# 22 of 36 modulation units moved from TensorE matmuls to multiply-adds on VectorE

## The reference

```python
c_act = jax.nn.silu(c)
for i in range(DEPTH):
    mod = (c_act @ mod_w[i] + mod_b[i]).reshape(B, N_SUBLAYERS, 3, D)
    shift, scale, gate = mod[:, :, 0], mod[:, :, 1], mod[:, :, 2]
    h = modulate(rms_norm(x, norm_g[i, 0]), shift[:, 0], scale[:, 0])
    x = x + 0.5 * gate[:, 0, None, :] * swiglu(h, w_gate[i, 0], w_up[i, 0], w_down[i, 0])
    ...
```

## Time and profile before

| | |
|---|---|
| median of 3 runs | 2283.04 us (2282.78 to 2283.24) |
| time of the profiled execution | 2281.24 us |
| its span | 2279.9 us |
| PE busy | 2187.2 us, 96% |
| DVE busy | 1365.1 us, 60% |
| ACT busy | 1095.2 us, 48% |
| moved by DMA | 448.64 MB, 197 GB/s on average |

### The profile page before, as it was taken

How to read it: one execution, slowest core, us unless ns; L and a number is a source line. 1 busy time by engine, 2 the same in 40 slices (tenths; PEclk the granted TensorE clock), 3 DMA queues, 4 the chain that set the end, 5 groups by cost and what they waited for, 6 DMA issues and landing times.

```text
span 2279.9 us, 33539 instructions
## 1 busy us (share of the span) xinstructions
PE 2187.2 (96%) x14432; PEld 1894.0 (83%) x14432; DVE 1365.1 (60%) x1776; ACT 1095.2 (48%) x1242; POOL 85.2 (4%) x92
## 2 busy tenths in 40 slices
PE   7999998999999999999899999999999999999998
PEld 5997665898789877678689987898999887998996
DVE  4543666654554466656665455567787664677884
ACT  4443555543444345545544335644555457445552
POOL 1200010000000000000000011000000111000000
PEclk9999999999999999999999999999999999999999
DMA  9776672656657655536265555444655564436551
GB/s 353 264 265 254 223 269 74 234 200 265 218 193 258 258 199 201 211 125 226 75 222 186 187 212 201 146 139 166 203 184 186 169 233 137 169 138 207 182 185 55
DMA packets 274819, 448.64 MB, mean 197 GB/s; under 512 B 10816, under 2 KB 146304, under 8 KB 274416
## 3 DMA queue, kind: packets, MB, share of 16 engines
q1 hardware_dynamic: 270016, 429.07, 54.5%
q0 software_dynamic: 4368, 16.31, 2.0%
q10 hardware_dynamic: 288, 1.11, 0.1%
HBM read 445.40 MB, written 1.06 MB: 196 GB/s over the span
## 4 chain that ended last, share of the span: by engine, by line
PE 78%; ACT 5%; DVE 4%; issue 1%; DMA 0%; POOL 0%; ACTq 0%; SPq 0%; DVEq 0%; POOLq 0%
PE ps L1449 76%; DVE wlo L1875 1%; ACT whi L1670 1%; PE ps L1636 1%; PE ps L1603 1%; ACT S L1670 1%; ACT L1670 1%; ACT xs L1670 0%; PE ps L1593 0%; DMA raw<-in_fox_w_in 0%; ACT xhi L1670 0%; DVE S L2009 0%; DVE x L1911 0%; ACT PT L1670 0%; DVE xs L1904 0%
## 5 line engine op out<-in xcount | busy, mean ns | idle before, releaser
L1875 DVE TENSOR_TENSOR wlo<-raw,whi 128x2048 fp32r<-128x2048 f32 (+1 forms) x339 | 768.2, 2274 | 533.1 <-ACT whi L1670 532.8
L1670 ACT ACTIVATE whi<-raw 128x2048 fp32r<-128x2048 f32 (+1 forms) x339 | 640.8, 1895 | 412.6 <-PE ps L1449 370.9
L1449 PE MATMUL ps<-xhi,whi 128*128 128x256 f32 x2632 | 649.5, 287 | 8.4 <-DVE wlo L1875 3.5
L1449 PE MATMUL ps<-xhi,wlo 128*128 128x256 f32 x2632 | 642.8, 284 | 0.0
L1449 PEld LDWEIGHTS ps<-xhi,whi 128*128 128x128 f32 x2632 | 507.4, 193 | 26.4 <-issue 16.5
L1449 PEld LDWEIGHTS ps<-xhi,wlo 128*128 128x128 f32 x2632 | 507.6, 193 | 1.3 <-issue 1.0
L1449 PE MATMUL ps<-xlo,whi 128*128 128x256 f32 x2632 | 344.3, 283 | 0.1
L1449 PEld LDWEIGHTS ps<-xlo,whi 128*128 128x128 f32 x2632 | 327.6, 192 | 0.5 <-DVE xlo L1975 0.3
L1449 PE MATMUL ps<-whi,xhi 128*128 128x512 f32 x736 | 299.1, 406 | 17.3 <-ACT xhi L1670 11.0
L1449 PE MATMUL ps<-wlo,xhi 128*128 128x512 f32 x736 | 291.9, 397 | 0.0
L1449 PE MATMUL ps<-whi,hhi 128*128 128x512 f32 x528 | 209.5, 397 | 1.9 <-DVE rows L1899 1.0
(11 more groups left out here) (218 smaller groups left out, 1811.9 us busy)
## 6 DMA issues: line engine op xcount, KB each, us to landing
raw<-in_mod_w SPq DMA_DIRECT2D x72, 1024.0 KB, 8.1
raw<-in_w_in SPq DMA_DIRECT2D x52, 1024.0 KB, 4.9
raw<-in_ffn_w_gate SPq DMA_DIRECT2D x88, 512.0 KB, 5.9
raw<-in_ffn_w_up SPq DMA_DIRECT2D x88, 512.0 KB, 6.9
raw<-in_ffn_w_down SPq DMA_DIRECT2D x44, 1024.0 KB, 8.7
raw<-in_w_up SPq DMA_DIRECT2D x88, 512.0 KB, 4.8
raw<-in_dil_w_in SPq DMA_DIRECT2D x36, 1024.0 KB, 5.5
raw<-in_w_down SPq DMA_DIRECT2D x22, 1024.0 KB, 4.9
```

Source lines behind the costliest of these rows:

```text
L1449: return nc.tensor.matmul(o, lhs, rhs, start=start, stop=stop, skip_group_check=True)
L1670: return nc.scalar.activation(o, i, func, **kw)
L1875: V.tensor_tensor(wlo[:, s["c"], 0:s["n"]], raw[:, s["slot"], 0:s["n"]], whi[:, s["c"], 0:s["n"]].bitcast(F32), ALU.subtract).then_inc(sem ...
```

## The change

22 of the 36 units are no longer matmuls. Each of their pieces ("half" below) is used by DVE in four instructions, one a row block: the first of a unit multiplies 128 x 512 weights by the column of `csil` (`tensor_scalar`), the others multiply and add onto an accumulator (`scalar_tensor_tensor`). There are two accumulators `macc` by turns, which lie in `xs[:, 1, :]`. PE then sums the accumulator over the partitions: a shift or scale unit by four float32 matmuls with one column of ones, a gate unit by one with 128 columns of ones as before. The copy to `mrow` on ACT goes away for them, and so does the reduce on DVE.

The instructions of a half are queued up (`work`) and put behind the matmuls of pieces in the order of steps: two behind each `gateup` piece, three behind each `down`. The slot of a half is free after its fourth instruction. PE's sums are put one unit later (`acc_turns`).

The halves stand before the steps that they go with: one before each `gateup` but the first (q = 2 to 10 in stage (0,0)), and one before `down` 0, 1, 3, 4 and 6, as long as the stage has any. Stage (0,0) has seven such units, (0,1) and (1,0) seven each, (1,1) one. The mixers keep four and one units as matmuls behind their steps; the second mixer had five. The norms keep one each, as before.

The transposes of x wait for one half of `xs` at a time. Two tiles of the mixers (`ftm`, `rtm`) now share memory with others.

```diff
+        while pc["slot_free"] and pc["slot_free"][0] == "mod_acc" and self.count.get("mod_acc", 0) < pc["slot_free"][1]:
+            self.run_work(1)
         c = pc["c"] = self.n_conv % CONV
...
+        for entry in self.acc_turns:
+            entry[0] -= 1
+        while self.acc_turns and self.acc_turns[0][0] < 0:
+            self.acc_turns.pop(0)[1]()
+
+    def run_work(self, n=2):
+
+        for _ in range(min(n, len(self.work))):
+            self.work.pop(0)()
...
             self.used(pc, tok)
+            self.run_work()
             self.run_beside()
...
+    def mod_half(self, i, u, h):
+
+        pc = self.take()
+        self.used(pc, ("mod_acc", self.acc_named + 4))
+        self.acc_named += 4
+
+        def part(kk):
+            acc = self.recent_unit % 2
+            before = self.recent_acc if h or kk else self.acc_free[acc]
+            tok = self.recent_acc = self.ev("dve", "mod_acc")
+            self.add("mod_acc", acc=acc, h=h, kk=kk, slot=pc["slot"], landed=pc["landed"], before=before)
+            if h and kk == 3:
+                self.acc_turns.append([2 if self.in_down else 1,
+                                       lambda: self.mod_turn(i, u, (G3 if self.in_down else D3) - u % 2, tok, acc)])
+                self.recent_unit += 1
+
+        self.work += [lambda kk=kk: part(kk) for kk in range(4)]
...
             tok = self.down_step(q, pc, bank_free, ((0, 0), (0, 1), (1, 0), (1, 1)))
             self.used(pc, tok)
+            self.run_work(3)
             self.run_turns()
...
+        in_norm = {("ffn", 0, 1): (0, 16), ("ffn", 1, 0): (1, 6), ("ffn", 1, 1): (1, 16), ("mix", 0): (0, 11), ("mix", 1): (1, 14)}
+        on_vector = {(0, 0): [(0, u) for u in range(4, 11)], (0, 1): [(0, 17)] + [(1, u) for u in range(6)],
+                     (1, 0): [(1, u) for u in range(7, 14)], (1, 1): [(1, 17)]}
+        fill = {0: [(0, u) for u in range(12, 16)], 1: [(1, 15)]}
...
             for q in range(11):
                 if (i, j, q) not in ((0, 0, 0), (0, 0, 1)):
+                    if q:
+                        half()
                     step("gateup", i=i, j=j, q=q)
-                for m in at[q]:
-                    step("mod", i=m[0], u=m[1])
             for q in range(11):
+                if q in (0, 1, 3, 4, 6):
+                    half()
                 step("down", i=i, j=j, q=q)
...
                     for m in range(4):
-                        ins = nc.tensor.transpose(ps[:, s["bank"], m * P:(m + 1) * P], mrow[:, m * P:(m + 1) * P], ident[:, :])
+                        c = slice(m * P, (m + 1) * P)
+                        if s["acc"] is not None:
+                            ins = mm(ps[:, s["bank"], m:m + 1], macc[s["acc"]][:, c], ones[:, 0:1], m == 0, True)
+                        else:
+                            ins = nc.tensor.transpose(ps[:, s["bank"], c], mrow[:, c], ident[:, :])
...
                     for m in TURN_ORDER:
+                        q.wait_ge(s["ready"][m // 4])
...
+                elif k == "mod_acc":
+                    c = 4 * s["h"] + s["kk"]
+                    w, o = raw[:, s["slot"], 512 * s["kk"]:512 * s["kk"] + 512], macc[s["acc"]]
+                    q.wait_ge(s["landed"])
+                    q.wait_ge(("c_silu", 1))
+                    q.wait_ge(s["before"])
+                    if c:
+                        V.scalar_tensor_tensor(out=o, in0=w, scalar=csil[:, c, 0:1], in1=o, op0=ALU.mult,
+                                               op1=ALU.add).then_inc(sem["mod_acc"])
+                    else:
+                        V.tensor_scalar(o, w, csil[:, 0, 0:1], None, ALU.mult).then_inc(sem["mod_acc"])
```

More of the change, by code:

```diff
@@ L64, in __init__ @@
         self.mod_row_free = None
+        self.acc_free = [None, None]
+        self.acc_named = self.recent_unit = 0
+        self.work = []
+        self.acc_turns = []
+        self.in_down = False
         self.mod_ready = {}
@@ L272, in mod_turn @@
             tok = self.gate_ready[(i, sub, u % 2)] = self.ev("dve", "mod_col")
-            self.add("gate_spread", g=g, half=u % 2, bank=bank, bank_free=bank_free, mod_row=row, mod_turned=turned,
+            self.add("gate_spread", acc=acc, g=g, half=u % 2, bank=bank, bank_free=bank_free, mod_row=row, mod_turned=turned,
                      rows_in=(f"row_in{g}", self.rows_in[g]))
@@ L1008, in step, with half @@
             steps.append(dict(kind=kind, **kw))
[L1010 to L1013, removed]
+        in_norm = {("ffn", 0, 1): (0, 16), ("ffn", 1, 0): (1, 6), ("ffn", 1, 1): (1, 16), ("mix", 0): (0, 11), ("mix", 1): (1, 14)}
+        on_vector = {(0, 0): [(0, u) for u in range(4, 11)], (0, 1): [(0, 17)] + [(1, u) for u in range(6)],
+                     (1, 0): [(1, u) for u in range(7, 14)], (1, 1): [(1, 17)]}
+        fill = {0: [(0, u) for u in range(12, 16)], 1: [(1, 15)]}
         def ffn(i, j):
-            fl = list(fill.get(("ffn", i, j), []))
+            halves = [(*m, h) for m in on_vector[i, j] for h in range(2)]
+            def half():
+                if halves:
+                    k, u, h = halves.pop(0)
+                    step("mod_half", i=k, u=u, h=h)
             if (i, j) == (0, 0):
@@ L1019, in ffn @@
             else:
[L1020 to L1023, removed]
+                step("norm", i=i, s=2 * j, m=in_norm["ffn", i, j])
             for q in range(11):
                 if (i, j, q) not in ((0, 0, 0), (0, 0, 1)):
+                    if q:
+                        half()
                     step("gateup", i=i, j=j, q=q)
-                for m in at[q]:
-                    step("mod", i=m[0], u=m[1])
             for q in range(11):
+                if q in (0, 1, 3, 4, 6):
+                    half()
                 step("down", i=i, j=j, q=q)
-                if q < 5:
-                    for m in at[11 + q]:
-                        step("mod", i=m[0], u=m[1], bank=G3)
         def mix(i):
-            fl = list(fill[("mix", i)])
-            step("norm", i=i, s=1, m=fl.pop(0))
+            fl = list(fill[i])
+            step("norm", i=i, s=1, m=in_norm["mix", i])
             if i == 0:
@@ L1109, in stage_pieces @@
             self.piece_unit(a["mod_w"][i], 512 * u, kind="m")
+        elif k == "mod_half":
+            k0 = 4 * s["h"]
+            self.piece("m", [((4, 512), 0, 512, self.view(a["mod_w"][i], k0, k0 + 4, 512 * u, 512 * u + 512))])
         elif k == "gateup":
@@ L1299, in build @@
         csil = named("csil", [P, NC, 32])
-        mrow = named("mrow", [P, 512])
+        mod_rows = named("mrow", [P, 2, 512])
+        mrow = mod_rows[:, 0, :]
+        macc = [xs[:, 1, 512 * a:512 * a + 512] for a in range(2)]
         rope = named("rope", [P, 2, 2, 16])
@@ L1691, in act_program @@
                     q.wait_ge(s["row_free"])
[L1692 removed]
+                    act(mrow, ps[:, s["bank"], :], ACT.Copy).then_inc(sem["mod_row"])
                 elif k == "square":
@@ L1823, in act_program @@
                         scale=dk[:, 4, h:h + 1]).then_inc(sem["decay"])
-                    act(ret_tm[:, h % 2, :], flat(rel[:, 1, :, :], 0, 2), ACT.Exp, scale=dk[:, 4, 4 + h:5 + h]).then_inc(sem["decay"])
+                    act(mod_rows[:, h % 2, :], flat(rel[:, 1, :, :], 0, 2), ACT.Exp, scale=dk[:, 4, 4 + h:5 + h]).then_inc(sem["decay"])
                 elif k == "ret_gate":
@@ L1885, in dve_program @@
                     c0 = mod[:, 4 * u:4 * u + 4]
[L1886 to L1889, removed]
+                    sums = ps[:, s["bank"], 0:4]
+                    if s["acc"] is None:
+                        sums = c0
+                        V.tensor_reduce(c0, ps[:, s["bank"], :].rearrange("p (m g n) -> p m g n", m=4, g=4)[:, :, :, 0], AX.X,
+                                        ALU.add).then_inc(sem["mod_col"])
+                        q.wait_ge(s["mod_col"])
+                    V.tensor_tensor(c0, sums, modb[:, i, 4 * u:4 * u + 4], ALU.add).then_inc(sem["mod_col"])
                     if kind:
```

43 lines of the change are left out of this document (25 added, 18 removed).

## The result

| | before | after |
|---|---|---|
| median | 2282.93 us | 2454.66 us (2454.33 to 2458.26, 4 runs) |
| ratio | | 1.0756, 95% interval 1.0737 to 1.0774 |
| profiled execution, its span | 2281.24, 2279.9 us | 2454.94, 2453.3 us |
| PE busy | 2187.2 us, 96% | 2202.4 us, 90% |
| DVE busy | 1365.1 us, 60% | 1479.3 us, 60% |

The forecast was 2425 us, with 2345 to 2480 as its range. The order of work that it described is there, and its sum is 30 us short.

What follows compares the result with a forecast made beforehand. PE was taken as the bound before, the loop through the one load queue after. 2281.2 + 197 (waiting) - 56 (units gone) - 4 (transposes) + 5 (clock) = 2423, by the median 2425 us; range 2345 to 2480.

Steps and rivals of the forecast that it cites:

- The loop: `gateup`: a half's slot, the loads behind it, splits and multiply-adds close a loop of 17.3 us a step, against PE's 11.52.
- rival (b): `gateup`: the loop exists but its terms overlap more, about 14.5 us a step; 2321 us by the median; chance 0.08.
- `down`: First-block `down`: pieces wait for slots of halves; 31 us lost in stage (0,0), 24 each in (0,1) and (1,0).
- What PE gets back: On PE: 22 units leave, matmuls 44.7 us and transposes 5.5 us go, 13 new sums add 10.9 us.
- The sum of a shift or scale unit: On PE: four float32 matmuls with one column, eight instructions at the pitch of a transpose, 0.84 us.
- Rival (a): Whole kernel: loads keep up, slots released or splits placed otherwise than read; -43, so 2240 us; chance 0.11.
- PE's balance: On PE, whole kernel: matmuls -44.7, transposes -5.5, new sums +10.9, together -39.3 us.
- The multiply-add: On DVE: one of 512 columns takes 0.69 us, bounds 0.483 to 0.77; a half costs 2.66 on average.
- The landing of A: `gateup`: A, first of a step's two weight pieces, lands 8.0 us after the half's slot is released; bounds 7.0 to 8.8.
- The clock: PE's granted clock falls after each wait; hidden by DVE's chain in a step, some 1.6 us at three stage ends: +5.
- rival (c): PE's clock stays low through each step, 20.4 us a step; about +125, 2550 us; chance 0.06.
- The transposes: Transposes of x waiting for one half of `xs` at a time: -4 us, which could be 0.

Runs made afterwards that it cites:

- e1: Changed kernel, with SP issuing each half behind the next two weight pieces; order on DVE, ACT and PE unchanged: 2309.3 us.
- e2: Changed kernel, with all four multiply-adds of a half ahead of the split that used to be before them on DVE: 2256.5 us.
- e3: Changed kernel, with the multiply-adds after the first of a unit taking 32 of 512 columns, all waits and loads kept: 2396.3 us, measured once.
- e9: Changed kernel, with each half loading two of its four row blocks and the other two multiply-adds using the same blocks again: 2420.0 us.
- e6: Changed kernel, with PE's sum at the end of the last `gateup` put into another PSUM bank, nothing else: 2453.6 us, measured once.
- e5: Kernel with the multiply-adds first, plus PE's sum at the end of the last `gateup` put into a bank not in use: 2239.4 us.
- e10: Changed kernel, with the split of the next stage's first weight piece planned during the tail, not ahead of it, in the first block: 2439.1 us.
- e8: Changed kernel, with each half loading two of its four row blocks and the other two multiply-adds using what lies in the slot: 4228 us, once.

## Why the prediction was right, point by point

**The loop.** Right, and shown from both sides: in the `gateup` parts it goes with the order of loads alone (e1), and everywhere with DVE's order alone (e2); and two of its terms were shortened by themselves (e3 the multiply-adds, e9 the load of the half). In the turn shown above, A landed 8.2 us after the release (forecast 8.0, which came from one place in the first mixer), `wlo` was done at 12.4 (12.25), the turn took 17.6 (17.3). So rival (b), a turn of 14.5, did not come.

**`down`.** Right to about a microsecond. Counted from the release at 193.99 in stage (0,0), the first four splits to matter were done, or their matmuls began, at 11.9, 23.8, 41.6 and 53.7 us (forecast 11.9, 23.9, 41.5, 53.5); `d6` began at 68.9 (67.8), the last split ended at 90.6 (89.4). The wait for the bank before the first `down` I had not seen. It had no price here that a single run shows (e6).

**What PE gets back.** The sum of a shift or scale unit, taken as 0.84 us without a row for it, held: in e2's timeline a step's pieces lie 6.64 apart with a sum in between, so the sum costs 0.88.

```profile
137.75 2.08 PE L1503 MATMUL ps<-xlo,whi 128*128 128x256 f32 x16
139.67 0.95 PE L1503 MATMUL ps<-ones,xs 128*128 128x1 f32 x8
144.39 2.08 PE L1503 MATMUL ps<-xlo,whi 128*128 128x256 f32 x16
```

Rival (a) gave 2240 us for a kernel in which the loads keep up; e5 is such a kernel, at 2239.4, which is 41.6 less than the kernel before beside it, where -43 was forecast. So PE's balance of -39.3, the 2.03 us of a unit's matmuls in it, holds as a total.

**The multiply-add.** Mis-sized: 0.750 us, where I took 0.69, inside the bounds of 0.483 to 0.77. That is 0.2 us a turn, 5 us over the 23 turns of the `gateup` parts and 2 in `down`.

**The landing of A.** Mis-sized too. Over the 23 turns it came 8.1 to 9.7 us after the release, 8.6 on average, where one place in the first mixer gave 8.0; in one turn of stage (0,1), released at 493.24, it came at 502.93:

```profile
494.20 8.73 DMA raw<-in_ffn_w_up
```

The mean turn over the three stages is thus 17.9 and not 17.3. That is 14 us of the missing 30, of which 5 are the multiply-adds. Why some loads landed later is open.

**The end of a stage.** Here the sum lacks a term, and with the longer turns this makes up nearly all of the missing 30 us. I followed the loop to the last `down` and let the tail follow PE. But the tail stands on DVE behind the split of the next stage's first piece, and that piece loads behind the slot of the last half. From the last `down` matmul to the norm's second transposes it was 5.1 us in each of the three stages before; after the change it is 12.6, 8.7 and 8.3, so 14 us more. e10 moves the split, and it is 7.2, 4.9 and 4.9: what is left of the wait is in (0,0).

**The clock.** As forecast, it falls after nearly every wait of PE in the loop and rises within the step, so rival (c) did not come. Over the stretches above it is 0.88; around the wait of 4.9 us that ends at 100.2 (columns as above):

```profile
100.00:102.00 2.00, 1.82 (x8) 1.85 (x9) 1.96 (x4) 1.11 (x2) 0.00 (x0) 0.53 0.04 8
102.00:104.00 2.00, 2.00 (x13) 2.00 (x12) 2.00 (x2) 0.00 (x0) 0.00 (x0) 0.61 0.00 0
104.00:106.00 2.00, 2.00 (x19) 2.00 (x18) 1.97 (x4) 0.00 (x0) 0.00 (x0) 1.00 0.02 5
```

The first wait of each stage is an exception: there the matmuls went on 0.12 apart. Part of a turn's surplus over 11.5 us is thus slow matmuls and not standing still: PE stood for 4.0 us a turn in (0,1), where the prediction had 5.8. No run separates the clock's price; in the loop it lies in the time that PE would wait anyway. In e2, where PE set the pace, part of the 17 us that e5 gave back is matmuls 0.43 apart after the wait. The Trainium skill (TensorE: Matmul & The Clock Gate, Why this matters for your kernels) warns of such idle gaps; the trace agrees: granted clock 0.53 and 0.61 in the rows above. But in the loop it was the late splits that set the pace, not the clock.

**The transposes.** Forecast -4, measured -3.2 alone.

## What to carry to other kernels

When a consumer is moved to another engine, follow its buffer first: who frees the slot now, what stands ahead of that instruction in its queue, and what is loaded behind that slot. Here 22 units of matmuls cost 44.7 us of PE, and the engine that took them over had time for them; but the slot was freed by an instruction that waited for a load that waited for the slot. If such a loop is there, add up its terms once; where the sum is above the pace of the bound engine, it is the new pace, and no engine will look full: here PE 78% and DVE 48% of the `gateup` stretch. To cut it, either free the slot earlier or move the load that waits for it behind those that need not wait. Here the first was enough by itself (2256.5 us); the second was enough in the `gateup` parts, but left some 70 us behind them (2309.3 against 2239.4 for e5).

## What the runs showed of the hardware that was not expected

- A multiply-add with a column operand over 128 x 512 float32, all in SBUF, takes 0.750 us, 0.06 more than an addition or subtraction of two such tensors (0.693).
- A float32 matmul with one column of ones shows as two instructions, and four of them cost PE 0.88 us in a dense stretch, twice the four transposes of the same tile (0.42).
- One run (e8) had all matmuls at about half pace from end to end (0.22 us a matmul of 256 columns) with a granted clock of 1.00 in the view; a nearly equal kernel later did not. For such a run the pitch of the matmuls is to be looked at, not the clock column.
